# Hybrid encoder trunk: the list of expert passes made in three groups, slots without register loads, first narrow loads behind the split

## The reference, cut to what matters

```
def moe_swiglu(h, router_w, router_b, w_gate, w_up, w_down):
    t = h.reshape(B * S, D)                       # 256 x 1024
    logits = (t @ router_w) + router_b
    top_v, top_i = lax.top_k(logits, 2)           # 2 of 8 experts for each token
    gates = jax.nn.softmax(top_v, axis=-1)
    combine = jnp.sum(jax.nn.one_hot(top_i, 8) * gates[..., None], axis=1)
    for e in range(8):                            # each: 3 matrices of 1024 x 3584
        out = out + combine[:, e:e + 1] * swiglu(t, w_gate[e], w_up[e], w_down[e])
```

## Time and profile before

| | us |
|---|---|
| time, median of 3 runs (1326.75 to 1327.37) | 1327.11 |
| the profiled execution's own time | 1327.16 |
| its span | 1325.3 |
| busy in the span: TensorE | 1192.7 |
| VectorE | 682.2 |
| ScalarE | 528.4 |

### The profile page before, as it was taken

The page is one execution under the profiler, slowest core; times in us unless marked ns, Lnnn a source line. Parts: engine busy times, 40 slices in busy tenths (PEclk is TensorE's granted clock), DMA queues, the critical chain, the costliest instruction groups (busy, mean ns, idle before and its releaser), DMA issues.

```text
span 1325.3 us, 18715 instructions
## 1 busy us (share of the span) xinstructions
PE 1192.7 (90%) x6925; PEld 855.2 (65%) x6925; DVE 682.2 (51%) x1021; ACT 528.4 (40%) x801; POOL 85.2 (6%) x123
## 2 busy tenths in 40 slices
PE   9999999999999899999999998778887787787785
PEld 8888888888978688888888874334434333343332
DVE  5996666667768889999999951000000000000002
ACT  4177444445757778877787840000000000000001
POOL 1000000001225000100010000000000000000000
PEclk9999999999999999999999999999999999999998
DMA  9612355554644989999999999999999999999996
GB/s 356 246 33 99 123 191 190 191 191 159 214 147 168 424 340 378 343 387 390 351 393 360 388 324 422 407 414 423 408 422 416 409 422 416 407 421 414 420 422 260
DMA packets 61689, 427.04 MB, mean 322 GB/s; under 512 B 7263, under 2 KB 7391, under 8 KB 11582
## 3 DMA queue, kind: packets, MB, share of 16 engines
q1 hardware_dynamic: 57470, 412.79, 78.5%
q0 software_dynamic: 4000, 13.42, 3.6%
q10 hardware_dynamic: 160, 0.04, 0.0%
HBM read 418.62 MB, written 7.60 MB: 322 GB/s over the span
## 4 chain that ended last, share of the span: by engine, by line
PE 56%; DMA 34%; DVE 5%; ACT 3%; issue 1%; DVEq 0%; POOL 0%; SPq 0%; POOLq 0%; ACTq 0%
DMA ring<-in_expert_blocks 34%; PE bank L1221 31%; PE bank L1270 6%; PE bank L1149 4%; PE bank L1537 4%; PE bank L1273 3%; PE bank L1169 2%; PE bank L1558 2%; DVE wl L1819 1%; ACT wh L817 1%; PE bank L1075 1%; PE bank L1520 1%; PE bank L1205 1%; ACT prob L897 0%; PE bank L1424 0%
## 5 line engine op out<-in xcount | busy, mean ns | idle before, releaser
L1819 DVE TENSOR_TENSOR wl<-ring,wh 128x1024 fp32r<-128x1024 f32 x338 | 405.2, 1225 | 28.6 <-ACT wh L817 12.3
L817 ACT CAST wh<-ring 128x1024 fp32r<-128x1024 f32 x338 | 350.7, 1056 | 81.1 <-PE bank L1221 77.4
L1537 PE MATMUL bank<-ring,R 128*64 128x256 f32 x2240 | 273.9, 388 | 70.0 <-DMA ring<-in_expert_blocks 69.8
L1537 PEld LDWEIGHTS bank<-ring,R 128*64 128x64 f32 x2240 | 159.5, 137 | 188.6 <-DMA ring<-in_expert_blocks 84.5
L1221 PE MATMUL bank<-wh,both 128*128 128x512 f32 (+1 forms) x768 | 237.1, 391 | 6.6 <-DVE wl L1819 6.3
L1026 ACT ACTIVATE R<-bank 128x256 f32<-128x256 f32 x35 | 13.4, 384 | 434.5 <-PE bank L1537 434.5
L1558 PE MATMUL bank<-ring,R 128*64 128x512 f32 x560 | 134.7, 603 | 35.0 <-DMA ring<-in_expert_blocks 30.8
L1221 PEld LDWEIGHTS bank<-wh,both 128*128 128x128 f32 x768 | 142.2, 189 | 36.8 <-issue 7.0
L2182 DVE COPY R<-bank 128x256 f32<-128x256 f32 x35 | 14.8, 424 | 274.1 <-PE bank L1544 274.1
L1221 PE MATMUL bank<-wl,both 128*128 128x512 f32 (+1 forms) x384 | 148.8, 388 | 0.0
L1270 PE MATMUL bank<-both,wh 128*128 128x512 f32 x352 | 110.7, 396 | 1.4 <-DVE both L1847 1.1
(11 more groups left out here) (301 smaller groups left out, 1116.8 us busy)
## 6 DMA issues: line engine op xcount, KB each, us to landing
ring<-in_expert_blocks SPq DMA_DIRECT2D x336, 1024.0 KB, 15.1
ring<-in_trunk_units SPq DMA_DIRECT2D x55, 1024.0 KB, 4.8
bias<-bias_scratch POOLq DMA_DIRECT2D x16, 128.0 KB, 3.2
token_rows<-prob POOLq DMA_DIRECT2D x3, 512.0 KB, 10.3
sum_rows<-X POOLq DMA_DIRECT2D x3, 512.0 KB, 21.6
X<-in_x SPq DMA_DIRECT2D x2, 512.0 KB, 4.4
X<-sum_rows POOLq DMA_DIRECT2D x2, 512.0 KB, 9.8
out<-X SPq DMA_DIRECT2D x4, 256.0 KB, 2.1
```

The source lines that it names most:

```text
L817: sa.copy(wh[:, place(n, h), :], ring_half(n, h)).then_inc(wh_ready, 1)
L1537: mm = pe.matmul(bank[NARROW * c:NARROW * c + NARROW, 0:S], x_n[:, k, :], w[:, q, c * S:(c + 1) * S], start=(k == 0), stop=(k == DC - 1))
L1819: ve.tensor_tensor(wl[:, place(n, h), :], ring_half(n, h), wh[:, place(n, h), :].bitcast(F32), ALU.subtract).then_inc(wl_ready, 1)
```

## The change

Four things change.

- `list_passes` takes a step. Its operations are the same; the first three run behind `gate_up` of block 1, the next three behind that of block 2, the last six behind that of block 3, and its wait for `table_ready` stands behind `gate_up` of block 4.
- In the opening pass `slots` moves from block 2 to 4, `take_rows` from block 3 to 5, and TensorE's `slot_rows` from block 3 to 5.
- `slots` loads only the expert into a register. The starts of the two ranges are read as scalars from `tabf`, added to `iota[:, 0:64]` in the same operation that compares.
- SyncE's loads of the first narrow pass are written out ahead of the loop, and its first seven wait for the split instead of the product.

```diff
--- before.py
+++ after.py
@@ -517,6 +517,9 @@
             def multiplied(old, i):
                 product_done(sp, old, i)
 
+            def first_narrow(old, i):
+                (split if old < U_MOE else multiplied)(old, i)
+
 
             load_pass(0, 0, split)
             sp.wait_ge(table_ready, 1)
@@ -525,7 +528,9 @@
             with sp.Fori(1, wides) as i:
                 e = sp.value_load(tab[0:1, bass.ds(i, 1)], min_val=0, max_val=E - 1)
                 load_pass(i, e, split)
-            with sp.Fori(wides, passes) as i:
+            e = sp.value_load(tab[0:1, bass.ds(wides, 1)], min_val=0, max_val=E - 1)
+            load_pass(wides, e, first_narrow)
+            with sp.Fori(wides + 1, passes) as i:
                 e = sp.value_load(tab[0:1, bass.ds(i, 1)], min_val=0, max_val=E - 1)
                 load_pass(i, e, multiplied)
 
@@ -1588,7 +1593,7 @@
                     expert_in(i, "g", b)
                     transpose_act(i, b - 1)
                     expert_in(i, "u", b)
-                    if b == 3:
+                    if b == (5 if opening else 3):
                         slot_rows(i + 1)
                     if b == 1 and not opening:
                         pe.wait_ge(y_ready, 2 * i)
@@ -2052,12 +2057,11 @@
             def slots(i):
 
                 e = ve.value_load(tab[0:1, bass.ds(i, 1)], min_val=0, max_val=E - 1)
-                r0 = ve.value_load(tab[0:1, bass.ds(i + T_FIRST, 1)], min_val=0, max_val=P)
-                r1 = ve.value_load(tab[0:1, bass.ds(i + T_SECOND, 1)], min_val=0, max_val=P + NARROW)
                 for t in range(TT):
-                    for a, r in enumerate((r0, r1)):
-                        ins = ve.tensor_scalar(pick[:, t, a * NARROW:(a + 1) * NARROW], iota[:, bass.ds(r, NARROW)],
-                                               rankm[:, t, bass.ds(e, 1)], None, ALU.is_equal)
+                    for a, start in enumerate((T_FIRST, T_SECOND)):
+                        ins = ve.tensor_scalar(pick[:, t, a * NARROW:(a + 1) * NARROW], iota[:, 0:NARROW],
+                                               tabf[:, bass.ds(i + start, 1)], rankm[:, t, bass.ds(e, 1)], ALU.add,
+                                               ALU.is_equal)
                 ins.then_inc(slots_ready, 1)
                 ve.tensor_copy(token_cols[:, :, 2:3], comb[:, :, bass.ds(e, 1)]).then_inc(cols_ready, 1)
 
@@ -2118,31 +2122,39 @@
                     xs = X[:, t, half * HALF:(half + 1) * HALF]
                     ve.tensor_tensor(xs, PB[banks[half]][:, :], xs, ALU.add).then_inc(o_added, 1)
 
-            def list_passes():
-
-                link(ve.tensor_tensor(same, spread(turn.rearrange("p (a n) -> p a n", a=1), 1, LISTED),
-                                      spread(iota[:, 1:1 + LISTED].rearrange("p (i a) -> p i a", a=1), 2, FLAGS),
-                                      ALU.is_equal))
-                link(ve.tensor_reduce(in_wide, same[:, :, 0:2 * E], AX.X, ALU.add))
-                link(ve.tensor_reduce(in_any, same[:, :, 0:E], AX.X, ALU.add))
-                link(ve.tensor_reduce(in_narrow, same[:, :, 2 * E:3 * E], AX.X, ALU.add))
-                link(ve.tensor_tensor(same, same, spread(expert_no.rearrange("p (a n) -> p a n", a=1), 1, LISTED), ALU.mult))
-                link(ve.tensor_reduce(tabf[:, T_EXPERT:T_EXPERT + LISTED], same, AX.X, ALU.add))
-                link(ve.tensor_tensor(in_any, in_any, in_narrow, ALU.add))
-                link(ve.tensor_scalar(tabf[:, T_FIRST:T_FIRST + LISTED], in_any, -float(P), float(P), ALU.mult, ALU.add))
-                link(ve.scalar_tensor_tensor(out=tabf[:, T_SECOND:T_SECOND + LISTED], in0=in_wide, scalar=float(NARROW),
-                                             in1=tabf[:, T_FIRST:T_FIRST + LISTED], op0=ALU.mult, op1=ALU.add))
-                link(ve.tensor_tensor(tabf[:, T_PASSES:T_PASSES + 1], tabf[:, T_PASSES:T_PASSES + 1],
-                                      tabf[:, T_FINAL:T_FINAL + 1], ALU.max))
-                link(ve.tensor_scalar(tabf[:, T_FINAL:T_FINAL + 1], tabf[:, T_PASSES:T_PASSES + 1], -1.0, None, ALU.add))
-                ve.tensor_copy(tab[:, 0:T_WIDES + 1], tabf[:, 0:T_WIDES + 1]).then_inc(table_ready, 1)
-                ve.wait_ge(table_ready, 1)
-
-            def next_slots(i, b):
-
-                if b == 2:
+            def list_passes(step):
+
+                if step == 0:
+                    link(ve.tensor_tensor(same, spread(turn.rearrange("p (a n) -> p a n", a=1), 1, LISTED),
+                                          spread(iota[:, 1:1 + LISTED].rearrange("p (i a) -> p i a", a=1), 2, FLAGS),
+                                          ALU.is_equal))
+                    link(ve.tensor_reduce(in_wide, same[:, :, 0:2 * E], AX.X, ALU.add))
+                    link(ve.tensor_reduce(in_any, same[:, :, 0:E], AX.X, ALU.add))
+                elif step == 1:
+                    link(ve.tensor_reduce(in_narrow, same[:, :, 2 * E:3 * E], AX.X, ALU.add))
+                    link(ve.tensor_tensor(same, same, spread(expert_no.rearrange("p (a n) -> p a n", a=1), 1, LISTED),
+                                          ALU.mult))
+                    link(ve.tensor_reduce(tabf[:, T_EXPERT:T_EXPERT + LISTED], same, AX.X, ALU.add))
+                elif step == 2:
+                    link(ve.tensor_tensor(in_any, in_any, in_narrow, ALU.add))
+                    link(ve.tensor_scalar(tabf[:, T_FIRST:T_FIRST + LISTED], in_any, -float(P), float(P), ALU.mult,
+                                          ALU.add))
+                    link(ve.scalar_tensor_tensor(out=tabf[:, T_SECOND:T_SECOND + LISTED], in0=in_wide,
+                                                 scalar=float(NARROW), in1=tabf[:, T_FIRST:T_FIRST + LISTED],
+                                                 op0=ALU.mult, op1=ALU.add))
+                    link(ve.tensor_tensor(tabf[:, T_PASSES:T_PASSES + 1], tabf[:, T_PASSES:T_PASSES + 1],
+                                          tabf[:, T_FINAL:T_FINAL + 1], ALU.max))
+                    link(ve.tensor_scalar(tabf[:, T_FINAL:T_FINAL + 1], tabf[:, T_PASSES:T_PASSES + 1], -1.0, None,
+                                          ALU.add))
+                    ve.tensor_copy(tab[:, 0:T_WIDES + 1], tabf[:, 0:T_WIDES + 1]).then_inc(table_ready, 1)
+                elif step == 3:
+                    ve.wait_ge(table_ready, 1)
+
+            def next_slots(i, b, at=2):
+
+                if b == at:
                     slots(i + 1)
-                if b == 3:
+                if b == at + 1:
 
                     ve.wait_ge(gate_moved, i + 1)
                     ve.wait_ge(idx_moved, i + 1)
@@ -2159,15 +2171,17 @@
                 act_low(i, 0)
                 split_low(i, "d", 0)
                 gate_up(i, 1)
+                if opening:
+                    list_passes(0)
                 for b in range(2, EB):
                     split_low(i, "g", b)
                     split_low(i, "u", b)
                     act_low(i, b - 1)
                     split_low(i, "d", b - 1)
                     gate_up(i, b)
-                    if b == 2 and opening:
-                        list_passes()
-                    next_slots(i, b)
+                    if opening:
+                        list_passes(b - 1)
+                    next_slots(i, b, 4 if opening else 2)
                 low_parts(expert_at["d", EB - 1, 0], i)
                 act_low(i, EB - 1)
                 take_xg(i + 1)
```

## The result

The changed kernel takes 1318.32 us (median of 6 runs, 1317.86 to 1319.85) against 1327.07 us for the kernel before beside it (6 runs, 1326.75 to 1327.37). The ratio is 0.9937 with a 95% interval of 0.9924 to 0.995: 8.75 us less, by the interval 6.6 to 10.1. The profiled execution took 1317.94 us with a span of 1316.2, 9.1 less than before. Forecast were 9.0 us and 1318.2.

What follows compares the result with a forecast made beforehand. VectorE's list stalls TensorE in the opening pass; the narrow stretch is bound by DMA, so starting it earlier moves the end. 7.13 + 1.04 + 0.8 = 9.0 us off 1327.16 gives 1318.2, range 1314.8 to 1321.5 (8 in 10).

Steps and rivals of the forecast that it cites:

- The allowance: Behind gate_up in wide passes: VectorE can be away 0.91 us for nothing; each us beyond costs TensorE one.
- Opening pass: List in three groups loses 1.24 us instead of 8.37: gain 7.13 us, bounds 4.4 and 8.37.
- `slots` in the later passes: Two of three register loads go: 0.52 us gained in each of two wide passes, 1.04 together, bounds 0 and 1.04.
- Transition: First narrow loads: seven issued earlier, the eighth unchanged but landing 0.6 us sooner; 0.8 us taken, at most 1.6.
- The half clock: Opening pass, behind TensorE's wait of 5.93 us: 2.4 of the 8.37 us lost are due to half clock.
- a clock that falls at each short wait: Rival, opening pass: three short waits each bring 2.4 us of half clock, so it gains nothing; 1325.3 us; chance 0.05.
- The weights: Opening pass, units 18 to 22 wanted some 7 us sooner: 3.0 us of lead holds; nothing put, bounds 0 and 3.
- The gather: Next pass's rows, fetched in block 5 of the opening pass instead of 3: 10.6 us of cover, costs nothing.

Runs made afterwards that it cites:

- the seventh alone: The kernel before with the first narrow pass's loads written out and only the seventh waiting for the split, all others for products; 1327.68 us, ratio 1.0009.
- The kernel one block later: The changed kernel with slots in block 5 and the fetch of rows in block 6 of the opening pass; 1327.71 us, ratio 1.0 to the kernel before.
- the kernel with slots only: The kernel before with slots reading the two starts as scalars from memory instead of loading registers, nothing else; 1324.92 us, ratio 0.9984.

## Why the prediction was right, point by point

**What bounds it.** VectorE's absence from the splits in the opening pass. The experiment with the list in one piece and that with six give the same work at 3.01 and 0 us, so it isn't the amount but the length of each absence. The clock is the smaller part: filling the wait with idle matmuls gave back 2.17 us of 8.37.

**The allowance.** It was the one number under most of the sum, read from `slots` in the kernel before as 0.91 us. Here is the time from the end of `gate_up` to the next split against what the block lost over 16.80 us, worked out from the rows above:

| kernel and place | absence, us | loss, us | difference |
|---|---|---|---|
| changed, group 1 | 1.28 | 0.43 | 0.85 |
| changed, group 2 | 1.41 | 0.56 | 0.85 |
| changed, group 3 | 1.02 | 0.16 | 0.86 |
| changed, slots | 0.88 | 0.03 | 0.85 |
| list in one piece | 3.89 | 3.01 | 0.88 |
| before, wait filled (to 462.73) | 7.07 | 6.20 | 0.87 |

From 0.9 to 7 us one line fits: all beyond 0.86 us is lost, each us once. In the blocks with `slots` of the later passes the same difference comes out between 0.81 (changed kernel, third pass) and 0.91 (the one that the prediction read), so the number is good to 0.05, and the prediction's was at the upper end. Groups two and three were shorter than reckoned (1.41 and 1.02 instead of 1.50 and 1.19): their first operation starts 0.08 to 0.09 us before the record of `gate_up` ends, and the last of group three runs 0.09 into the split. The loss came out as 1.15 us instead of 1.24. Why the allowance is 0.86 stays open: no run changed how many halves may wait (`SPLITS`) or how large they are.

**The terms.** Opening pass 7.13 forecast, 7.17 measured. That it hits to 0.04 is luck: the 8.37 us from which it starts hold a half clock that cost 1.84 to 2.77 us in four executions of the same code, so against another execution of the kernel before the gain would be 6.8 to 7.8. `slots` in the later passes 1.04 forecast, 0.94 measured in its two blocks. The idle time went as said, while a comparison with two scalars, taken at 0.25 us, takes 0.31 and used up what was left of the allowance. Transition 0.8 forecast, 0.9 in this pair of executions, 0.3 to 1.1 over all that was run; the forecast's bounds of 0 and 1.6 hold, and the near hit is luck.

The working for that last term doesn't stand. The eighth load isn't earlier, as said. But it was to land 5.4 us behind its issue in the kernel before (784.11 to 789.5) and 4.8 in the changed one, 0.6 less; it took 8.5 and 5.4, 3.1 less, and most of that was gone by the eighteenth load. And by that working the seventh load decides, while with the seventh alone nothing came. The loads came 1.9 to 4.4 us earlier in the kernel with this edit alone, not 2 to 3.

**The half clock.** 2.4 us were put down to it; it was 2.17 in that execution and 1.84 to 2.77 over four. Its rival, a clock that falls at each short wait, is refuted: TensorE waits 0.3 us at most for VectorE's splits in the opening pass, and the granted clock is 1.00 in both of its stretches, 413 to 464 and 464 to 530 us.

**The weights.** No wait of ScalarE or TensorE for a load appeared in the opening pass; the cover held.

**The gather.** It did cost nothing, but the cover was reckoned too wide: 10.6 us forecast, 7.7 measured, since this gather took 10.5 us instead of the 7.1 of the one read before. The kernel one block later shows that this is the edit's real risk.

## What to carry to other kernels

Small serial work on an engine that feeds the bound one is paid by the piece, not by the sum: read from any block that has such work what the loss is, subtract it from the absence, and the rest is the allowance. Cut everything to pieces below that allowance, at every place that has one. A long wait also costs what the clock gives up behind it, here 1.8 to 2.8 us behind one of 5.9 and nothing behind one of 2.76. When work is put off, count what its last consumer needs, with the longest transfer in the trace and not the nearest (the same gather took 7.1, 9.8 and 10.5 us here), and ask of an earlier load which later one still waits for the same event.

## What the runs showed of the hardware

- TensorE's granted clock was 0.50 behind waits of 4.88 us (the kernel with slots only, 464 to 466 us), 5.93 and 8.29 us, and stayed at 1.00 behind waits of 2.76 and 0.3 us. Behind the same wait of 5.9 us the half clock cost 1.84 to 2.77 us in four executions.
- A float32 matmul of 128 columns is two records in the trace; 44 of them took 9.99 us, 0.227 us each, as much as one of 512 columns on the split parts (fp32r). A float32 transpose of 128 columns is one record, 0.13 us.
- Three register loads on VectorE left it idle for 2.35 us behind a table just written, one for 1.07; where the table had long been written, three left 0.61 to 0.70 and one none.
